# Masked attentions of a two-block transformer: TensorE takes the units of work in twos

## The chip, the cores and the metric

The program runs on one core of one Trainium2 chip. The metric is the device time of one execution, in microseconds (us). Five engines work beside each other, each through its own list of instructions in order, and they wait for one another by counting semaphores: TensorE (PE; its weight loads are shown apart as PEld), VectorE (DVE), ScalarE (ACT), GpSimd (POOL) and SyncE (SP, which issues DMAs).

## The reference, cut to what matters

Two transformer blocks run one after the other over 512 tokens of width 1024. Nearly all of their work is matrix products with weights. Two stages are masked attentions, and the change touches these alone. The first has 16 heads of 64 columns:

```
logit[t,s] = q_t.k_s / sqrt(d) + c[t] - c[s]   for s <= t, else -1e30
pr = softmax(logit);   o = pr @ v              # 512 tokens, 16 heads of 64
```

The second (`moba_attention`) has 8 heads of 64. At 512 tokens and blocks of 256 it comes to a plain causal softmax with a bias of slope times distance. A third attention, over a memory of 256 tokens and without a mask, has code of its own and is not touched.

## The kernel before, in words

A program writes the instruction list of each engine by hand. Weights come by DMA in slabs into `raw`. ScalarE rounds them to `w_hi`, GpSimd makes the rest `w_lo`, and TensorE does three products for each (lines 599 to 601). Outside the attentions TensorE is fed in this way without a break.

A masked attention is cut into units. Unit `i` is one pair of heads `j = i // 4` and one tile of 128 queries `qb = ROW_TILE[i % 4]`, with `ROW_TILE = (0, 3, 1, 2)`. As the mask is causal, its keys are the first `qb + 1` blocks of 128, so that units 0, 1, 2, 3 of a pair have 1, 4, 2 and 3 blocks. The first attention has N = 32 units and the second 16. Each unit has two halves, `hh` 0 and 1, one head each. Its way through the engines:

- `S_(i)` on TensorE (line 853): the scores of both heads, each on 64 rows of the array (line 863), then for each head a bf16 product that adds the mask (line 865) and tells `scored`. Odd units write banks 0 and 1 of `gp`, even ones banks 0 and 1 of `ms`. It waits until the maxima of unit i-2 are there (`biased`).
- `B_(s)` on VectorE (line 1897), for each half `s = 2 * i + hh`: bias added, row maximum taken. `E_(s)` on ScalarE (line 1346): exponential and row sum.
- `R_(i)` on VectorE (lines 1904 and 1908): reciprocal of the sums and scaling of both halves, which tells `weighted`.
- `T_(i)` on TensorE (line 874): for each half one transpose a block into bank 2 + hh of `ms`. Half 0 waits for `weighted` and until half 0 of unit i-1 was copied out of that bank; half 1 waits until half 1 of unit i-1 was.
- `C_(s)` on ScalarE (line 1354): that copy, into one of the four buffers `probT`.
- `V_(i)` on TensorE (line 885): the products with the values, each head on 64 columns of the array, after both copies of unit i. `H_(j)` and `L_(j)` on ScalarE and VectorE (lines 1358 and 1551) take a finished pair of heads out of PSUM.

What order VectorE and ScalarE keep is fixed and is not part of the change. VectorE does for each i: both `B_` of unit i, then `R_(i-1)`, and every fourth time an `L_`. ScalarE takes for each i the copies of unit i-3 and the exponentials of unit i in turn, half by half:

```
def C_(s):
    act.wait_ge(transposed, t0 + s + 1)
    if s >= 4:
        act.wait_ge(pv_done, at["pv"] + s // 2 - 1)
    act.activation(probT[s % 4][:, 0:w], ms[:, 2 + s % 2, 0:w], ACT.Copy).then_inc(pt_copied, 1)
for i in range(N + 3):
    for s in (2 * i, 2 * i + 1):
        if i >= 3: C_(s - 6)
        if i < N: E_(s)
    if i >= 8 and i % 4 == 0: H_(i // 4 - 2)
```

So ScalarE's order is C(u) half 0, E(u+3) half 0, C(u) half 1, E(u+3) half 1, and a copy of unit u waits also for `V_(u-2)`, which must have read the buffer that it overwrites. VectorE's `B_` of unit i waits in addition for the transposes of unit i-4, which read the place that it writes.

TensorE's order before is `S_(i)`, `T_(i-3)`, `V_(i-4)` for each i.

Of the kernel before, what the change touches and what calls it, by code (L numbers as in the profile page):

```python
# [116 lines left out]
def build(nc, hbm, out):  # L117
# [74 lines left out]
    with ExitStack() as ctx:  # L192
# [393 lines left out]
        def wait_evac(eng, pos, c):  # L586
            eng.wait_ge(evac[pos.slot(4, c)], pos.turns(4, c) + 1)
# [3 lines left out]
        def _(pe):  # L591
# [253 lines left out]
            def head_attention(at, n, queries, keys, values, before):  # L845

                t0, N = at["step"], 4 * n

                def S_(i):
                    j, qb = i // 4, ROW_TILE[i % 4]
                    w, bank = (qb + 1) * P, (ms, gp)[i % 2]
                    if i == 1:
                        for c in range(2):
                            wait_evac(pe, before, c)
                    if i >= 2:
                        pe.wait_ge(biased, t0 + 2 * i - 2)  # L860
                    for hh in range(2):
                        r = slice(64 * hh, 64 * hh + 64)
                        pe.matmul(bank[:, hh, 0:w], queries[r, j, qb * P:qb * P + P], keys[r, j, 0:w], start=True, stop=False)
                    for hh in range(2):
                        pe.matmul(bank[:, hh, qb * P:w], identb[:], tri[:], start=False, stop=True).then_inc(scored, 1)

                def T_(i):
                    for hh in range(2):
                        s = 2 * i + hh
                        pe.wait_ge(weighted, at["weighted"] + s + 1)  # L870
                        if i:
                            pe.wait_ge(pt_copied, at["pt"] + s - 1)
                        for kb in range(ROW_TILE[i % 4] + 1):
                            m = pe.transpose(ms[:, 2 + hh, kb * P:kb * P + P], prob_of[2 * ROW_TILE[i % 4] + hh][:, kb * P:kb * P + P], ident[:])
                        m.then_inc(transposed, 1)

                def V_(i):
                    j, qb = i // 4, ROW_TILE[i % 4]
                    pe.wait_ge(pt_copied, at["pt"] + 2 * i + 2)
                    if i % 4 == 0 and j >= 2:  # L880
                        pe.wait_ge(lo_done, at["split"] + j - 1)
                    for kb in range(qb + 1):
                        for hh in range(2):
                            c = j * P + 64 * hh
                            m = pe.matmul(gp[64 * hh:64 * hh + 64, 2 + j % 2, qb * P:qb * P + P], values[:, kb, c:c + 64],  # L885
                                          probT[(2 * i + hh) % 4][:, kb * P:kb * P + P], start=(kb == 0), stop=(kb == qb),
                                          skip_group_check=True)
                    m.then_inc(pv_done, 1)

                for i in range(N + 4):  # L890
                    if i < N:
                        S_(i)
                    if 3 <= i < N + 3:
                        T_(i - 3)
                    if i >= 4:
                        V_(i - 4)

            head_attention(fox, 8, qT, kT, v_s, Pos(gv["blk"] + 4))
            gemm(wo, A, ready=fox["split"])
            ffn_layer(1, B, A)  # L900
# [91 lines left out]
            slabs_wide(gvm, A, 0)  # L992
            branch(0, 0, lru["split"], 4)
            head_attention(mob, 4, qm, km, vm, Pos(br[0]["blk"] + 12))
            branch(1, 4, mob["split"], 4, late=2)
            first_blocks(wout, A, mrg["split"])
# [1312 lines left out]
```

## Time and profile before

| | |
|---|---|
| time, median of 3 runs | 2130.27 us (2128.96 to 2130.34) |
| span of the profiled execution (first to last instruction) | 2127.2 us |
| PE busy | 2098.9 us, 99% of the span |
| PEld / DVE / ACT / POOL busy | 1705.7 / 1014.4 / 805.4 / 936.1 us |
| mean granted TensorE clock | 0.997 of full speed |
| first masked attention, from its first score product to the first product of the next stage | 762.92 to 839.57 |
| second one | 1570.84 to 1612.62 |

The profile gives no time of its own for the profiled execution beside the span; what lies around the span is the difference to the runs, 3.1 us at the median. Busy time of PE is modelled at the ends of its instructions, so the distance from one start to the next is the surer measure of what a step takes. A time in brackets at the end of a row is the idle time of that engine ahead of the row, with what ended it.

### The profile page before, as it was taken

The page shows a single profiled execution, that of the slowest core. Times are in us where ns is not written, and L with a number is a line of the kernel's source. Part 1 is how long each engine was busy: PE and PEld are TensorE (multiplying, and loading weights), DVE is VectorE, ACT ScalarE, POOL GpSimd, SP SyncE. Part 2 cuts the span into 40 slices and gives each one's busy share as a digit, 9 for nine tenths or more (in the row PEclk, how much of TensorE's full clock was granted, in tenths as well). Part 3 has the DMA queues.
Part 4 walks back from the last instruction along what each step waited for, and adds up shares of the span by engine and source line. Part 5 has one row for each costly group of instructions (what it writes and reads, how often), then busy time and mean ns, then how long its engine had stood idle before and what let it go on. Part 6 is the DMA issues. An engine that isn't in the chain of part 4 may idle for free.

```text
span 2127.2 us, 26516 instructions
## 1 busy us (share of the span) xinstructions
PE 2098.9 (99%) x9908; PEld 1705.7 (80%) x9908; DVE 1014.4 (48%) x1580; ACT 805.4 (38%) x1243; POOL 936.1 (44%) x436
## 2 busy tenths in 40 slices
PE   9999999999999999999999999999999999999998
PEld 7777888888888866888888887878867888888887
DVE  7996623122356555532132355572454466254463
ACT  7766322122343157322222355352244343232232
POOL 5984544444444410444444442444443444444442
PEclk9999999999999999999999999999999999999999
DMA  5332432222222222232222221222211222322221
GB/s 193 133 115 79 145 113 82 96 100 97 99 81 99 100 90 90 80 117 81 100 97 99 99 91 49 104 82 98 98 60 60 99 90 97 106 84 100 97 99 60
DMA packets 33803, 205.31 MB, mean 97 GB/s; under 512 B 4512, under 2 KB 6688, under 8 KB 10672
## 3 DMA queue, kind: packets, MB, share of 16 engines
q1 hardware_dynamic: 33424, 199.87, 26.6%
q10 hardware_dynamic: 288, 4.19, 0.5%
q8 instruction: 60, 0.98, 0.2%
q14 instruction: 31, 0.25, 0.0%
HBM read 197.73 MB, written 6.32 MB: 96 GB/s over the span
## 4 chain that ended last, share of the span: by engine, by line
PE 60%; issue 23%; POOL 10%; DVE 5%; ACT 1%; DMA 0%; POOLq 0%; SPq 0%; DVEq 0%; ACTq 0%
PE gp L599 19%; PE gp L600 19%; PE gp L601 18%; POOL w_lo L493 9%; DVE ms L1554 3%; POOL pool_sum L516 1%; DMA h<-x_hbm 0%; PE gp L646 0%; PE gp L645 0%; PE gp L647 0%; PE ms L742 0%; PE ms L737 0%; PE gp L945 0%; PE gp L885 0%; DVE acc_sq L1551 0%
## 5 line engine op out<-in xcount | busy, mean ns | idle before, releaser
L493 POOL TENSOR_TENSOR w_lo<-raw,w_hi 128x1024 fp32r<-128x1024 f32 x350 | 848.0, 2426 | 1099.2 <-ACT w_hi L1071 1077.5
L599 PE MATMUL gp<-a_hi,w_hi 128*128 128x512 f32 (+1 forms) x1456 | 567.4, 390 | 1.8 <-DVE a_lo L1554 0.9
L601 PE MATMUL gp<-a_hi,w_lo 128*128 128x512 f32 (+1 forms) x1456 | 563.2, 387 | 0.0
L600 PE MATMUL gp<-a_lo,w_hi 128*128 128x512 f32 (+1 forms) x1456 | 563.1, 387 | 0.0
L1071 ACT ACTIVATE w_hi<-raw 128x1024 fp32r<-128x1024 f32 x349 | 365.5, 1051 | 505.9 <-PE gp L601 434.2
L600 PE MATMUL gp<-b_lo,w_hi 128*128 128x512 f32 (+1 forms) x1216 | 469.7, 386 | 0.0
L599 PE MATMUL gp<-b_hi,w_hi 128*128 128x512 f32 x1184 | 462.8, 391 | 0.0
L601 PE MATMUL gp<-b_hi,w_lo 128*128 128x512 f32 x1184 | 460.6, 389 | 0.0
L599 PEld LDWEIGHTS gp<-a_hi,w_hi 128*128 128x128 f32 x1456 | 273.5, 188 | 60.3 <-POOL w_lo L493 1.5
L600 PEld LDWEIGHTS gp<-a_lo,w_hi 128*128 128x128 f32 x1456 | 273.5, 188 | 56.5 <-issue 1.4
L601 PEld LDWEIGHTS gp<-a_hi,w_lo 128*128 128x128 f32 x1456 | 273.4, 188 | 55.5
L1551 DVE TENSOR_TENSOR h<-gp,h 128x512 f32<-128x512 f32 (+1 forms) x106 | 72.1, 681 | 424.4 <-PE gp L601 424.4
L600 PEld LDWEIGHTS gp<-b_lo,w_hi 128*128 128x128 f32 x1216 | 228.4, 188 | 47.2 <-issue 1.2
L599 PEld LDWEIGHTS gp<-b_hi,w_hi 128*128 128x128 f32 x1184 | 222.3, 188 | 47.5 <-issue 1.0
L601 PEld LDWEIGHTS gp<-b_hi,w_lo 128*128 128x128 f32 x1184 | 222.3, 188 | 46.0
L1551 DVE TENSOR_TENSOR T<-gp,rstd 128x512 f32<-128x512 f32 x136 | 93.8, 690 | 308.7 <-PE gp L601 306.4
L1554 DVE SCALAR_TENSOR_TENSOR ms<-u_pad,par,ms 128x512 f32<-128x512 f32 x176 | 120.1, 749 | 1.2 <-ACT ms L1144 0.4
L1080 ACT ACTIVATE sqb<-h 128x512 f32<-128x512 f32 x61 | 38.4, 631 | 130.2 <-DVE h L1551 116.3
L1554 DVE SCALAR_TENSOR_TENSOR T<-gpad,par,T 128x512 f32<-128x512 f32 x48 | 83.3, 1734 | 5.2 <-DVE T L2131 0.2
L1272 ACT ACTIVATE b_hi<-U 128x512 fp32r<-128x512 f32 x32 | 20.3, 634 | 121.3 <-DVE U L1554 121.3
L1272 ACT ACTIVATE a_hi<-U 128x512 fp32r<-128x512 f32 x32 | 20.3, 634 | 120.6 <-DVE U L1554 120.6
L516 POOL TENSOR_TENSOR pool_sum<-pool_sum,sqb 128x512 f32<-128x512 f32 x45 | 57.2, 1290 | 8.5 <-ACT sqb L1163 8.3
(333 smaller groups left out, 1829.0 us busy)
## 6 DMA issues: line engine op xcount, KB each, us to landing
raw<-w_hbm SPq DMA_DIRECT2D x176, 1024.0 KB, 4.8
proj_scratch<-kT ACTq DMA_DIRECT2D x2, 2048.0 KB, 6.7
fbias<-negc_scratch SPq DMA_DIRECT2D x16, 256.0 KB, 3.4
h<-x_hbm SPq DMA_DIRECT2D x4, 512.0 KB, 7.5
u_pad<-proj_scratch SPq DMA_DIRECT2D x1, 2048.0 KB, 10.1
big<-proj_scratch SPq DMA_DIRECT2D x1, 2048.0 KB, 8.7
out_hbm<-h SPq DMA_DIRECT2D x8, 256.0 KB, 2.2
mem_raw<-mem_hbm SPq DMA_DIRECT2D x1, 1024.0 KB, 12.5
```

The lines of the kernel that those rows point to most:

```text
L493: g.tensor_tensor(at(w_lo), src, f32(at(w_hi)), ALU.subtract).then_inc(w_lo_done, 1)
L516: g.tensor_tensor(pool_sum[:, s], pool_sum[:, s], product_at(i, s, t + 1), ALU.add).then_inc(pool_conv, 1)
L599: pe.matmul(o, wh, xh, start=start, stop=False)
L600: pe.matmul(o, wh, xl, start=False, stop=False)
L601: return pe.matmul(o, wl, xh, start=False, stop=stop)
L1071: act.activation(at(w_hi), src, ACT.Copy).then_inc(w_hi_done, 1)
L1080: act.activation(dst, h[:, c], ACT.Square).then_inc(sq_done, 1)
L1272: act.activation(H_[0][:, k], U[:, k % 2], ACT.Copy).then_inc(hi_done, 1)
L1551: return v.tensor_tensor(o, a, b, op)
L1554: return v.scalar_tensor_tensor(o, a, s, b, op0, op1)
```

## The change

Only TensorE's order of the calls changes; the calls themselves, their waits and the lists of the other engines stay.

```
-                for i in range(N + 4):
-                    if i < N:
-                        S_(i)
-                    if 3 <= i < N + 3:
-                        T_(i - 3)
-                    if i >= 4:
-                        V_(i - 4)
+                for i in range(3):
+                    S_(i)
+                for i in range(0, N, 2):
+                    T_(i)
+                    for a in (i + 3, i + 4):
+                        if a < N:
+                            S_(a)
+                    T_(i + 1)
+                    if i:
+                        V_(i - 1)
+                    V_(i)
+                V_(N - 1)
```

For even i the order is now `T_(i)`, `S_(i+3)`, `S_(i+4)`, `T_(i+1)`, `V_(i-1)`, `V_(i)`. Both masked attentions use this function.

## Rows read from the trace of the kernel before

**Rows 1.** Busy time of each engine by stretch: engine, busy us, instructions; granted clock; DMA.
```profile
762.92:839.57 76.65, 73.15 (x673) 45.72 (x672) 58.31 (x232) 63.77 (x200) 2.35 (x1) 1.00 0.13 43
1570.84:1612.62 41.78, 37.53 (x338) 22.90 (x337) 32.87 (x117) 31.25 (x99) 4.17 (x4) 1.00 0.01 2
762.90:772.00 9.10, 7.32 (x49) 3.57 (x48) 7.82 (x33) 7.49 (x24) 2.35 (x1) 1.00 0.10 33
2124.00:2127.20 3.20, 0.00 (x0) 0.00 (x0) 0.00 (x0) 0.00 (x0) 0.00 (x0) 0.88 0.74 250
```

**Rows 2.** Timeline of PE, first attention: start us, length us, engine, line, operation.
```profile
791.92 0.70 PE L863 MATMUL ms<-kT,qT 64*128 64x256 f32 x4
...
795.41 0.39 PE L874 MATMUL ms<-ident,T 128*128 128x128 f32 x2
795.73 0.88 PE L885 MATMUL gp<-sqb,v_s 128*64 128x128 f32 x12
796.53 0.49 PE L863 MATMUL ms<-kT,qT 64*128 64x128 f32 x4
796.96 0.29 PE L865 MATMUL ms<-tri,identb 128*128 128x128 bf16 x2
...
798.42 1.13 PE L863 MATMUL gp<-kT,qT 64*128 64x512 f32 x4
799.49 0.28 PE L865 MATMUL gp<-tri,identb 128*128 128x128 bf16 x2
799.61 0.61 PE L874 MATMUL ms<-ident,U 128*128 128x128 f32 x4
800.14 1.09 PE L885 MATMUL gp<-sqb,v_s 128*64 128x128 f32 x16
801.17 0.70 PE L863 MATMUL ms<-kT,qT 64*128 64x256 f32 x4
```

**Rows 3.** Timeline of the same stretch: ScalarE, one step of VectorE, one of PE.
```profile
792.17 0.72 ACT L1346 ACTIVATE T<-T,nmax 128x512 f32<-128x512 f32 x1 [1.00 <-DVE nmax L1897]
...
792.90 0.36 ACT L1354 ACTIVATE acc_sq<-ms 128x256 f32<-128x256 f32 x1
...
793.40 0.52 PE L874 MATMUL ms<-ident,T 128*128 128x128 f32 x3 [0.22 <-DVE T L1908]
...
794.73 0.48 ACT L1354 ACTIVATE sqb<-ms 128x384 f32<-128x384 f32 x1
795.10 0.51 ACT L1346 ACTIVATE U<-U,nmax 128x256 f32<-128x256 f32 x1
...
795.74 0.56 DVE L1897 CUSTOM_DVE_ANT_0 T<-gp,fbias 128x384 f32<-128x384 f32 x1 [0.58 <-PE ms L874]
...
796.34 0.62 ACT L1346 ACTIVATE T<-T,nmax 128x384 f32<-128x384 f32 x1 [0.34 <-DVE nmax L1897]
...
797.73 0.60 ACT L1354 ACTIVATE sqb<-ms 128x512 f32<-128x512 f32 x1
...
798.22 0.39 ACT L1346 ACTIVATE T<-T,nmax 128x128 f32<-128x128 f32 x1
```

**Rows 4.** Timeline of the first steps of the first attention.
```profile
763.34 0.29 PE L865 MATMUL ms<-tri,identb 128*128 128x128 bf16 x2
...
763.56 1.13 PE L863 MATMUL gp<-kT,qT 64*128 64x512 f32 x4
763.77 0.29 DVE L1897 CUSTOM_DVE_ANT_0 T<-ms,fbias 128x128 f32<-128x128 f32 x1
...
767.38 0.39 PE L874 MATMUL ms<-ident,T 128*128 128x128 f32 x2
...
767.72 0.49 PE L863 MATMUL ms<-kT,qT 64*128 64x128 f32 x4
```

**Rows 5.** Timeline of the last products with the values and the step after them.
```profile
838.77 0.88 PE L885 MATMUL gp<-sqb,v_s 128*64 128x128 f32 x12
...
839.69 0.60 ACT L1358 ACTIVATE a_hi<-gp 128x512 fp32r<-128x512 f32 x1 [0.98 <-PE gp L885]
```

## The prediction

> **What bounds the kernel now.** I read the busy times of the page first: PE is busy for 99% of the span, so that a change of TensorE's order counts one for one as soon as it opens a gap. Then the stretches of the two masked attentions [rows 1]: 76.65 us and 41.78 us, PE busy for 73.15 and 37.53 of them, with ACT at 63.77 in the first, which is close behind. Then the timeline of PE in the steady part [rows 2]: one pair of heads (four units) goes from the score product at 791.92 to the one at 801.17, 9.25 us. All other stages are untouched, and their weights are fetched ahead, so the whole difference must come from 12 such groups of four units, 8 in the first attention and 4 in the second.
>
> The prices of TensorE's steps, from start to start [rows 2]. Scores: 0.43 us for one block (796.53 to 796.96) and 1.07 for four (798.42 to 799.49), so 0.213 a block and 0.216 before the mask may start. Transposes of both halves: 0.32 for one block each (795.41 to 795.73), 0.53 for two, so 0.108 a transpose and 0.105 before the values start. Values: 0.80 for three blocks, 1.03 for four (800.14 to 801.17), so 0.213 a block and 0.17 after them. The two mask products: 0.11, and 0.01 to the transposes. Four units hold 10 blocks: scores 2.13, values 2.13, 20 transposes 2.16, eight mask products 0.44, together 6.86. The changes between kinds of products add 4 x (0.216 + 0.105 + 0.17 + 0.01) = 2.00. That is 8.86, and the missing 0.39 is a wait that the trace shows. At 793.40 half 1 of a three-block transpose starts after a gap [rows 3]. The row names a scaling on VectorE as the releaser, but that one was long done. What ended last is the copy of the unit before: the copy at 792.90 takes 0.36, and 0.11 later PE goes on. That copy stood behind the exponential of 792.17, and this behind a maximum of VectorE (1.00 idle, ended by it). This pattern decides the case: **ScalarE's half-1 copy of unit u stands behind the exponential of unit u+3**, so it needs the scores of unit u+3.
>
> **What the change does to TensorE alone.** No instruction is added or removed, no DMA is moved. Per two units the old order has S-mask, T-V and V-S twice each. The new one has S-mask twice, and T-S, mask-S, T-V and V-T once each. The trace shows mask-S: the mask at 763.34, the next score product at 763.56, so 0.22 less 0.11 for the mask, 0.11 [rows 4]. T-S it shows once, 767.38 to 767.72, 0.34 less two transposes, 0.12, where a wait may be in it; so it lies between 0 and 0.12, and I take 0.11, near the row. V-T I take as V-S, 0.17, between 0 and 0.2; it doesn't matter below, since a wait covers it. Per four units the changes then cost 0.86 + 0.22 + 0.22 + 0.21 + 0.34 + 0.02 = 1.87 in place of 2.00. So packing the like products together saves 0.13 us in four units, 1.6 us in all.
>
> The Trainium skill's page TensorEngine Tiling (Array Packing), section Tiling Modes, Key Properties, says that a change of the tiling mode, and not merely of the tile, drains TensorE. By its rule one counts borders between modes: the full-array mask stands between the two score products, so there are six borders per two units in the old order and six in the new, and the saving would be nothing in place of 1.6 us.
>
> **What it does to the waits.** Take the new order for even i: T(i), S(i+3), S(i+4), T(i+1), V(i-1), V(i), and write h0 and h1 for the halves.
>
> First, S(i+3) used to be issued ahead of T(i) and now comes after it. The copy of T(i) h1 stands behind the exponential of unit i+3, and T(i+1) h1 can't start before that copy. So PE, having done S(i+3), S(i+4) and T(i+1) h0, stands still until the way scores, maximum, exponential, copy has been walked through.
>
> Second, a copy of unit i+1 waits for V(i-1), and V(i-1) used to be issued ahead of T(i+1). Now it comes after it. So these copies can't begin while V(i-1) runs, and T(i+2), which comes next but for V(i), waits for both of them, with the exponential of unit i+4 h0 between the two.
>
> These two chains join end to end, and nothing of them runs beside itself. Prices: from the start of a mask to the maximum 0.43 (763.34 to 763.77, rows 4), taken as 0.44. From a maximum to its exponential its length and 0.11: 0.60 for three blocks (795.74 to 796.34, rows 3), 0.73 for four (VectorE steps grow by 0.13). An exponential holds ScalarE for 0.38, 0.49, 0.61, 0.72 by blocks. A copy holds it for 0.37 at three blocks (794.73 to 795.10) and 0.49 at four (797.73 to 798.22), taken as 0.48; with the time to PE it is its length (0.26, 0.38, 0.48, 0.58) and 0.11 [rows 3]. From the end of V to a copy 0.28: at 838.77 three blocks take 0.64, and ScalarE starts at 839.69 [rows 5]. I take it between 0.17, what PE itself needs after V, and 0.35, as much above.
>
> Now one period of four units, i = 0 mod 4, from the start of the h0 copy of unit i-1 (three blocks):
> - copy 0.37, exponential of i+2 0.49, h1 copy to PE 0.59, T(i) h1 and change 0.22, scores of i+3 (three blocks) 0.855, to the maximum 0.44, to the exponential 0.59, exponential 0.61, h1 copy of i (one block) to PE 0.37, T(i+1) h1 (four blocks) and change 0.535, V(i-1) three blocks 0.64, to the copy 0.28: 5.99 us;
> - h0 copy of i+1 0.48, exponential of i+4 0.38, h1 copy to PE 0.69, T(i+2) h1 and change 0.33, scores of i+5 (four blocks) 1.07, 0.44, 0.73, exponential 0.72, h1 copy of i+2 to PE 0.49, T(i+3) h1 and change 0.43, V(i+1) four blocks 0.85, 0.28: 6.88 us.
>
> Together **12.87 us in place of 9.25**. As a check from PE's side: 8.73 of work and changes, and waits of 0.27 and 0.75 at T(i), 0.81 at T(i+1) h1, 0.59 and 0.64 at T(i+2), 1.07 at T(i+3) h1, 4.13 in all. The other queues keep clear of this path: VectorE has some 7.3 us of work in a period and ScalarE 7.5, H and L among them. The bias DMAs are issued a head pair ahead, as now. With the two open prices at their ends (T-S 0 or 0.12, V to copy 0.17 or 0.35, each twice), the period is 12.4 to 13.0.
>
> Start and end, rolled forward by the same terms: T(1) h1 at 7.29 us after the first score product, V(0) at 7.82, T(2) h1 at 9.24 behind the copies, S(5), its maximum, its exponential and the h1 copy of unit 2, T(3) h1 at 13.01 and V(1) at 13.44. Six periods of 12.87, a last one of 9.89 (no scores are left to wait for), and 2.76 to the end: 103.3 us for the first attention. The old order rolled in this way gives 9.21 a period and 76.2 in all, where the trace has 76.65, which is the best proof that I have for the prices. So +26.7. The second attention: 13.44 + 2 x 12.87 + 9.89 + 2.76 = 51.8. Its old roll is 39.4 against 41.78 in the trace, so 2.4 us there are of another kind (VectorE still busy with the stage before as it starts, and longer waits behind it). They may stay (+12.4) or be swallowed by the new waits (+10.0); I take +11.0. Sum +37.7 us. On the span of 2127.2 that is 2164.9, and as the median of the runs stands 3.1 above the span, **2168**. Own range: twelve periods at 12.4 to 13.0 and the two ends of the second attention's start give 2161 to 2171.
>
> **Rivals.**
> *The waits are hidden and only the packing counts* (the other side). The mechanism sits at the copies: if ScalarE reached them without the exponentials between, PE would run at 8.73 in four units against 9.21 to 9.25, about 0.5 x 12 = 6 us less: 2124. It decides where the waits in a period fall below 0.5 us. For it: PE is 95% busy in the stage now, and ACT has slack. Against it: the wait of 793.40 arises already now, with S(u+3) issued ahead of T(u).
> *Only the first chain bites*, because the end of V(i-1) frees the buffer soon enough. The same roll without that wait gives 10.79 a period, 88.0 and 44.9 us: +11.4 and about +4, 2146. For it: the three blocks are a short product. Against it: the program's wait stands between them without anything to cover it.
> *The clock falls.* PE would be idle for a third of the stage, in gaps up to 1.1 us. At half the clock (1.2 GHz in place of 2.4) the TensorE terms on the path, some 4.5 us of a period, double: 17.4, +50 us more, 2218. Against it: from 762.90 to 772.00 PE was busy for 7.32 of 9.10 and the clock stayed at 1.00; the only drop is 0.88 in the last 3.2 us, with PE wholly idle [rows 1]. The Trainium skill, TensorE: Matmul & The Clock Gate, in its section on a second failure mode (psum-queue depth-cycling), tells of a kernel whose short idle times between groups of products made the clock swing; so far the trace doesn't bear that out.
>
> **How the numbers follow.** The forecast gets 0.82, the hidden waits 0.06, the first chain alone 0.07, the clock 0.05. The range of 2154 to 2182 holds the forecast's own range with a margin for prices that I have mis-sized by a third of the added waits, and leaves the rivals out. A difference of 0.2% (4.3 us) is what can be told from none. Faster: 0.04; same: 0.03; slower: 0.93.
>
> **What would show it.** Right: four units take 12.4 to 13.0 us in the steady part of both attentions; the transposes show idle PE ahead of h1 four times in a period, the longest, about 1.1, ahead of the three-block unit; ScalarE's copies after odd units start about 0.3 after the three- or four-block value product; the clock stays 1.00 and all other stages keep their length. Wrong: a period under 11 with copies that start ahead of V's end would leave the first chain alone; a period near 8.8 without waits, the packing; transposes that last twice as long, the clock.

## The result, and the profile after

The changed kernel takes 2172.49 us (median of 5 runs, 2171.84 to 2174.56) against 2129.49 us before (5 runs): ratio 1.0205, interval 1.0194 to 1.0216. It is 43.0 us slower, where I had forecast 37.7. The span of its profiled execution is 2170.7 us, 43.5 more than before. Instructions and bytes are the same in number. PE's busy time grew by 8.8 us all the same. The profile models the ends of its instructions, so that two transposes followed by a wait are shown as 0.41 us, though the next step could begin after 0.22; so part of each wait counts as busy, and a stretch at half clock in the second attention adds to it. The rest of the difference is idle time.

First the row of the page with the busy times (share of the span, number of instructions), then the two attentions and two short stretches of the second one by windows (stretch and length; busy us of PE, PEld, DVE, ACT, POOL; granted clock; DMA share and GB/s):

```profile
PE 2107.7 (97%) x9908; PEld 1708.8 (79%) x9908; DVE 1015.4 (47%) x1580; ACT 805.2 (37%) x1243; POOL 936.6 (43%) x436
```

```profile
762.84:869.20 106.36, 77.41 (x673) 46.89 (x672) 58.87 (x232) 63.65 (x200) 2.35 (x1) 1.00 0.09 31
1600.47:1655.87 55.40, 40.40 (x338) 23.89 (x337) 33.16 (x117) 31.26 (x99) 4.17 (x4) 0.97 0.00 1
...
1607.00:1611.00 4.00, 1.63 (x13) 0.83 (x11) 3.86 (x12) 2.95 (x10) 2.09 (x2) 1.00 0.01 4
1611.35:1614.82 3.47, 3.47 (x11) 1.15 (x10) 0.95 (x3) 0.39 (x2) 0.00 (x0) 0.51 0.00 0
```

Against the first two of [rows 1] the attentions are 29.7 and 13.6 us longer, 43.3 of the 43.5 us. Everything else kept its length to 0.3 us. VectorE and ScalarE did the same work (DVE 58.87 us against 58.31, ACT 63.65 against 63.77): the engines stand and wait for each other.

One period of four units in the first attention, from the timeline (start, length, engine, line; in brackets the idle time ahead and its releaser; line numbers of ScalarE and VectorE are 5 higher than before):

```profile
791.65 0.48 ACT L1359 ACTIVATE sqb<-ms 128x384 f32<-128x384 f32 x1
...
792.27 0.30 PE L874 MATMUL ms<-ident,T 128*128 128x128 f32 x1 [0.57 <-ACT sqb L1359]
...
792.50 0.92 PE L863 MATMUL gp<-kT,qT 64*128 64x384 f32 x4
793.35 0.28 PE L865 MATMUL gp<-tri,identb 128*128 128x128 bf16 x2
793.57 0.49 PE L863 MATMUL ms<-kT,qT 64*128 64x128 f32 x4
793.80 0.56 DVE L1902 CUSTOM_DVE_ANT_0 T<-gp,fbias 128x384 f32<-128x384 f32 x1 [2.93 <-PE gp L865]
...
794.40 0.61 ACT L1351 ACTIVATE T<-T,nmax 128x384 f32<-128x384 f32 x1 [1.61 <-DVE nmax L1902]
...
795.01 0.26 ACT L1359 ACTIVATE acc_sq<-ms 128x128 f32<-128x128 f32 x1
...
795.41 0.63 PE L874 MATMUL ms<-ident,T 128*128 128x128 f32 x4 [0.69 <-DVE U L1913]
...
795.97 0.88 PE L885 MATMUL gp<-sqb,v_s 128*64 128x128 f32 x12
...
796.96 0.60 ACT L1359 ACTIVATE sqb<-ms 128x512 f32<-128x512 f32 x1 [1.09 <-PE gp L885]
...
798.57 0.41 PE L874 MATMUL ms<-ident,U 128*128 128x128 f32 x2 [0.46 <-ACT sqb L1359]
...
798.91 1.13 PE L863 MATMUL gp<-kT,qT 64*128 64x512 f32 x4
...
802.38 0.52 PE L874 MATMUL ms<-ident,T 128*128 128x128 f32 x3 [0.94 <-DVE T L1913]
802.83 1.09 PE L885 MATMUL gp<-sqb,v_s 128*64 128x128 f32 x16
...
804.03 0.49 ACT L1359 ACTIVATE sqb<-ms 128x384 f32<-128x384 f32 x1 [1.09 <-PE gp L885]
...
804.91 0.48 ACT L1359 ACTIVATE sqb<-ms 128x384 f32<-128x384 f32 x1
```

The same copy comes again 13.26 us later (791.65 to 804.91), where [rows 2] had 9.25 us. The reader can walk both chains. First chain: the scores of 792.50 come after the transpose of 792.27. The maximum starts at 793.80 after VectorE had been idle for 2.93, the exponential at 794.40, the copy at 795.01, and the transposes of 795.41 had waited for that copy. The row names VectorE's scaling for it, wrongly, as it did before. Second chain: the values of 795.97, then the copy at 796.96, which names PE as its releaser (1.09 idle). In [rows 2, 3] no copy waits for values.

### The profile page after: what moved, and what is told of

The parts are those of the page before. It is cut to its first block, busy times and chain, and to the rows that moved or that the text cites. A ratio compares the mean times of both kernels' runs of the same rounds, so it can differ in the third digit from the quotient of the medians.

```text
span 2170.7 us, 26516 instructions
## 1 busy us (share of the span) xinstructions
PE 2107.7 (97%) x9908; PEld 1708.8 (79%) x9908; DVE 1015.4 (47%) x1580; ACT 805.2 (37%) x1243; POOL 936.6 (43%) x436
## 4 chain that ended last, share of the span: by engine, by line
PE 59%; issue 24%; POOL 10%; DVE 5%; ACT 1%; DMA 0%; POOLq 0%; SPq 0%; ACTq 0%; DVEq 0%
PE gp L599 18%; PE gp L601 18%; PE gp L600 18%; POOL w_lo L493 9%; DVE ms L1559 3%; POOL pool_sum L516 1%; PE gp L885 0%; PE gp L863 0%; PE gp L647 0%; PE gp L645 0%; PE gp L646 0%; PE ms L737 0%; PE ms L742 0%; DMA h<-x_hbm 0%; PE ms L874 0%
## 5 line engine op out<-in xcount | busy, mean ns | idle before, releaser
L874 PE MATMUL ms<-ident,T 128*128 128x128 f32 x192 | 33.7, 281 | 29.7 <-DVE T L1913 10.6
```

## The experiments

Each ratio is to the kernel before, with its interval. First four runs cut or keep one chain each. A border is a change from one kind of product to another on TensorE; "borders" is the rival by which the new neighbours on TensorE cost the time.

**Eight buffers.** The changed order, but the copies go into eight buffers in place of four; the four new ones are tiles of `rest_of_b` that are free in both attentions, and the products with the values read from the same eight.

```
+        probT8 = probT + tuple(rest_of_b[:, k] for k in range(4))
-                    if s >= 4:
-                        act.wait_ge(pv_done, at["pv"] + s // 2 - 1)
-                    act.activation(probT[s % 4]...
+                    if s >= 8:
+                        act.wait_ge(pv_done, at["pv"] + s // 2 - 3)
+                    act.activation(probT8[s % 8]...
```

> The changed order, but the copies go into eight buffers instead of four (the four new ones lie in memory that is free in both attentions), so that a copy of unit u waits for the values of unit u-4 and no longer for those of unit u-2. My theory (two chains end to end): the second chain is cut. ScalarE's copies of odd units start right behind the transposes, a period of four units goes from 13.26 to about 10.85 us, and the kernel to about 2148 us, 24 less than the changed one. Rival (the new borders between kinds of products on TensorE cost the time, not the waits): no product has moved, so nothing changes, 2172 us.

Measured: 2150.33 us (4 runs), 1.0101 (1.0085 to 1.0118), 22 us less than the changed kernel. The timeline, a period:

```profile
793.28 1.13 PE L864 MATMUL gp<-kT,qT 64*128 64x512 f32 x4
...
797.20 1.09 PE L886 MATMUL gp<-sqb,v_s 128*64 128x128 f32 x16
797.22 0.47 ACT L1360 ACTIVATE rest_of_b<-ms 128x384 f32<-128x384 f32 x1
...
801.94 0.63 PE L875 MATMUL ms<-ident,T 128*128 128x128 f32 x4 [0.70 <-DVE U L1914]
...
804.23 0.70 PE L864 MATMUL gp<-kT,qT 64*128 64x512 f32 x2
```

10.95 us from 793.28 to 804.23. The copy of 797.22 starts with the values of 797.20 and no longer behind them. The wait of the first chain (0.70 at 801.94) is untouched. No product of TensorE has changed its place in the order, so borders fall as a cause for these 22 us, half of the loss.

**Copies first.** The changed order with four buffers, but ScalarE takes both copies of a unit before both exponentials:

```
-                    for s in (2 * i, 2 * i + 1):
-                        if i >= 3:
-                            C_(s - 6)
-                        if i < N:
-                            E_(s)
+                    if i >= 3:
+                        C_(2 * i - 6)
+                        C_(2 * i - 5)
+                    if i < N:
+                        E_(2 * i)
+                        E_(2 * i + 1)
```

> The changed order, but ScalarE takes both copies of unit u before both exponentials of unit u+3, instead of in turn. My theory: the first chain is cut (the half-1 copy no longer stands behind an exponential that needs the scores of unit u+3), and the second one is shortened by the exponential between its two copies. A period of about 10.3 us, 2143 us. Rival (borders): 2172 us. Second rival (ScalarE's queue is not the cause, VectorE's scaling is, as the trace names it): 2172 us too, with idle PE named for VectorE as before.

Measured: 2141.68 us (4 runs), 1.0058 (1.0041 to 1.0075). What is left:

```profile
795.99 0.83 PE L874 MATMUL ms<-ident,T 128*128 128x128 f32 x6
...
800.80 1.04 PE L874 MATMUL ms<-ident,T 128*128 128x128 f32 x8
...
802.76 1.09 ACT L1359 ACTIVATE sqb<-ms 128x512 f32<-128x512 f32 x2 [0.36 <-PE gp L885]
...
803.50 0.90 PE L874 MATMUL ms<-ident,U 128*128 128x128 f32 x4 [0.63 <-ACT sqb L1359]
```

The odd units' transposes, six and eight in a row, now run without a gap between their halves: the waits of 0.94 and 0.69 that had VectorE's name are gone, though nothing of VectorE was changed. So it was the copy, and the name was wrong. The second chain stands (0.36 ahead of the copies, 0.63 on PE).

**Only the values in twos**, order `S_(i+3)`, `T_(i)`, `S_(i+4)`, `T_(i+1)`, `V_(i-1)`, `V_(i)`; **only the scores in twos**, order `T_(i)`, `S_(i+3)`, `S_(i+4)`, `V_(i-1)`, `T_(i+1)`, `V_(i)`:

```
                 for i in range(0, N, 2):
+                    if i + 3 < N:
+                        S_(i + 3)
                     T_(i)
-                    for a in (i + 3, i + 4):
-                        if a < N:
-                            S_(a)
+                    if i + 4 < N:
+                        S_(i + 4)
                     T_(i + 1)
```
```
+                    if i:
+                        V_(i - 1)
                     T_(i + 1)
-                    if i:
-                        V_(i - 1)
                     V_(i)
```

> Only the half of the change that puts products with the values together: S(i+3), T(i), S(i+4), T(i+1), V(i-1), V(i). My theory: the second chain stays and the first is shorter, as S(i+3) stands ahead of T(i) again: a period of about 11.2 us, 2151 us. Rival (borders between kinds of products): this order has five borders per two units against six in the kernel before, so it would be no slower than 2129.5 us.

> Only the half of the change that puts scores together: T(i), S(i+3), S(i+4), V(i-1), T(i+1), V(i). V(i-1) stands ahead of T(i+1) again. My theory: the first chain stays, the second goes: a period of about 10.8 us, 2147 us, near the run with eight buffers. Rival (borders): seven borders per two units, one more than the changed kernel, so slower than 2172 us.

Measured: values alone 2155.34 us (4 runs), 1.0121 (1.0104 to 1.0138); scores alone 2149.74 us (4 runs), 1.0099 (1.0082 to 1.0115). By borders the first (five in two units, where the kernel before has six) had to beat the kernel before, and the second had to be the slowest of all. (My expectation counts seven borders for it; there are eight, as both `T_` now stand behind a `V_`.) Neither is so. Each half alone costs 20 to 26 us, so each has its own chain. The scores alone, period 10.84 us as expected:

```profile
794.67 1.13 PE L863 MATMUL gp<-kT,qT 64*128 64x512 f32 x4
...
805.51 1.13 PE L863 MATMUL gp<-kT,qT 64*128 64x512 f32 x4
```

The values alone missed by 4 us, and the profiled run, with 2159.44 us the slowest of its four, by 8. Steady periods in its first attention are 11.29, as expected, or 12.9 (once 13.1). The timeline of such a longer one, and windows: the attention, one us of the longer period, and four us behind the same step of the next period, which is a short one:

```profile
786.38 0.52 PE L874 MATMUL ms<-ident,T 128*128 128x128 f32 x3 [1.65 <-DVE T L1914]
786.83 1.69 PE L885 MATMUL gp<-sqb,v_s 128*64 128x128 f32 x16
789.30 1.53 PE L863 MATMUL gp<-kT,qT 64*128 64x384 f32 x4
```

```profile
763.42:861.59 98.17, 80.81 (x673) 51.10 (x672) 58.31 (x232) 64.20 (x200) 2.35 (x1) 0.93 0.10 33
789.00:790.00 1.00, 1.00 (x6) 0.51 (x4) 0.00 (x0) 1.00 (x5) 0.00 (x0) 0.50 0.00 0
799.29:803.29 4.00, 4.00 (x42) 2.72 (x43) 2.51 (x10) 2.77 (x10) 0.00 (x0) 1.00 0.00 2
```

After the idle 1.65 us, from shortly after 787 until shortly before 791, the granted clock is at 0.50, the lower level of 1.2 GHz. The three-block scores take 1.46 to their mask (789.30 to 790.76) in place of 0.85. The mean over this attention is 0.93, against 1.00 in the changed kernel. The idle 1.65 us do not bring the fall each time: the same idle time stands ahead of 799.29 and of 823.49, and behind both the clock stayed at 1.00 for the next 4 us. In this trace four of the first attention's six idle times of 1.65 are followed by a fall, and two in the second attention. The longest idle times of PE in the changed kernel, in its first and in its second attention:

```profile
861.96 0.63 PE L874 MATMUL ms<-ident,T 128*128 128x128 f32 x4 [1.33 <-DVE U L1913]
...
1611.01 0.41 PE L874 MATMUL ms<-ident,U 128*128 128x128 f32 x2 [1.61 <-DVE T L1913]
```

The clock stayed at 1.00 behind the first and fell behind the second. In the run with the scores alone two idle times of 1.61 stand in the second attention, and only behind the later one did the clock fall. So each fall seen in the attentions came behind an idle time of about 1.6 us; what else decides is not shown.

**Both chains cut** in the changed order (both diffs above):

> The changed order with both chains cut: eight buffers for the copies, and both copies of a unit ahead of both exponentials. My theory (the two chains are the whole cost): what is left is the way from S(i+3), now behind T(i), to the transposes two units on; a period of about 9.5 us, 2134 us. Rival (borders between kinds of products): 2172 us less what the two runs alone gave (22 and 31 us), so if each takes its own piece 2119 us, and if they overlap as two chains that share the exponential do, my figure.

Measured: 2131.80 us (10 runs), 1.0011 (1.0002 to 1.0021), period 9.54 us. 40.7 of the 43.0 us are back, with TensorE's order as in the changed kernel. The two alone gave 22 and 31, 53 in sum: they overlap, as two chains that share an exponential must. What is left of the waits, from the timeline:

```profile
798.90 0.62 ACT L1352 ACTIVATE T<-T,nmax 128x384 f32<-128x384 f32 x1 [0.97 <-DVE nmax L1904]
...
800.11 1.06 ACT L1360 ACTIVATE sqb<-ms 128x512 f32<-128x512 f32 x2
...
800.83 0.90 PE L875 MATMUL ms<-ident,U 128*128 128x128 f32 x4
...
801.65 1.13 PE L864 MATMUL gp<-kT,qT 64*128 64x512 f32 x4
```

The copies of unit i+1 (800.11) still stand behind the exponentials of unit i+3 (798.90), whose scores now come after `T_(i)`. The transposes of 800.83 wait for these copies and take 0.82 us to the next scores, where four transposes and the change are 0.54 by the prices of the prediction. Such waits come to 0.8 us in a period, 9.54 against the 8.73 of work and changes (an estimate by the same prices). The profile shows only 0.3 of them as idle time (PE is busy for 9.24 us of 9.54), since the modelled ends of its instructions cover the rest.

**The kernel before with copies first; the values in twos with both chains cut:**

> The kernel before, with both copies of a unit ahead of both exponentials on ScalarE. My theory: the wait of some 0.4 us in a period that the order before has (half-1 copy behind an exponential) goes, a period of 8.86 in place of 9.24 us: 3.3 us less in the first attention and 1.8 in the second, 2125 us. Rival (PE is busy 99% and that wait costs nothing, or it comes back in another place): 2129.5 us.

> Products with the values in twos, score products one by one as before (S(i+3), T(i), S(i+4), T(i+1), V(i-1), V(i)), with eight buffers and copies first, so that both chains are cut. My theory: five borders per two units where the kernel before has six, and no waits: a period of about 8.55 us against 8.86 for the old order with copies first; 2121 to 2122 us, the best of all. Rival (packing brings nothing, since what a border costs is a wait for weights that is there either way): not under the run with copies first, about 2125 us.

Measured: 2122.63 us (6 runs), 0.9969 (0.9957 to 0.9981), and 2121.08 us (5 runs), 0.9958 (0.9945 to 0.9972). Periods from the timelines, first of the old order, then of the values in twos:

```profile
797.11 1.13 PE L863 MATMUL gp<-kT,qT 64*128 64x512 f32 x4
805.94 1.13 PE L863 MATMUL gp<-kT,qT 64*128 64x512 f32 x4
```

```profile
796.93 1.13 PE L864 MATMUL gp<-kT,qT 64*128 64x512 f32 x4
...
800.17 1.09 PE L886 MATMUL gp<-sqb,v_s 128*64 128x128 f32 x16
801.09 0.61 PE L886 MATMUL gp<-rest_of_b,v_s 128*64 128x128 f32 x8
801.31 0.84 ACT L1361 ACTIVATE rest_of_b<-ms 128x384 f32<-128x384 f32 x2
801.63 0.92 PE L864 MATMUL gp<-kT,qT 64*128 64x384 f32 x4
...
805.46 1.12 PE L864 MATMUL gp<-kT,qT 64*128 64x512 f32 x3
```

8.83 and 8.53 us. So the wait that the kernel before already had was worth 0.4 us a period, and packing the values 0.30 more. The second run has eight buffers besides, which were not tried alone in the old order; but the 8.83 us are already what the old order's steps come to without any wait (8.86 by the prediction's prices), so more buffers had nothing to give there. The run with the old order is 2.4 us faster than I expected (2125). Its first attention is 3.6 us shorter (73.08 us), where I expected 3.3, and its second 3.2 (38.53 us), where I expected 1.8. Six blocks of values take 1.46 us to the next scores (800.17 to 801.63): 1.28 of work and 0.18, where two single ones pay 0.17 each.

**The bias rows ahead.** My roll of the second attention missed 2.4 us. GpSimd makes four of its eight bias rows while it runs. In this run of the kernel before all eight are made ahead of it, and ahead of GpSimd's next slabs of weights:

```
-                if j >= 2:
-                    g.wait_ge(biased, mob["step"] + 8 * (j - 1))
-                    g.tensor_tensor(mbias[:, r % 4], dist[:], ...
+                    g.tensor_tensor(mbias[r], dist[:], ...   # r of 8, in kT and rest_of_b
```

> The kernel before, with all eight bias rows of the second attention made by GpSimd before it starts, in memory that is free then, in place of four before and four during it. It tests what the 2.4 us of another kind are that my roll of the second attention missed: in the trace before, VectorE's scaling takes 2.20 us in place of 0.62 where GpSimd makes a bias beside it. Theory: the two slow steps go, the second attention is about 1.5 us shorter, 2128 us. Rival: the steps were slow for another reason, 2129.5 us.

Measured: 2128.18 us (11 runs), 0.9993 (0.9984 to 1.0002): not told from no change. Two rows from the changed kernel, GpSimd's bias and VectorE's scaling of 256 columns, and four from this run, the same two with two products of VectorE between them:

```profile
1607.41 2.09 POOL L564 TENSOR_TENSOR mbias<-dist,par 128x512 f32<-128x512 f32 x2 [8.52 <-DVE nmax L1902]
1607.45 2.20 DVE L1913 TENSOR_SCALAR U<-U,rinv 128x256 f32<-128x256 f32 x2
```

```profile
1562.65 1.04 POOL L562 TENSOR_TENSOR rest_of_b<-dist,par 128x512 f32<-128x512 f32 x1
...
1567.23 2.17 DVE L1549 TENSOR_TENSOR merged<-merged,T 128x512 f32<-128x512 f32 x1
...
1572.83 0.69 DVE L1549 TENSOR_TENSOR merged<-merged,T 128x512 f32<-128x512 f32 x1
...
1578.90 0.61 DVE L1906 TENSOR_SCALAR U<-U,rinv 128x256 f32<-128x256 f32 x2
```

2.20 us against 0.61: the mechanism is shown. The second attention is 40.57 us long against 41.78, 1.2 us of the 2.4. The two slow steps were worth more: the second and third period lost 0.80 and 1.13 us, but the first grew by 0.74. For GpSimd's slabs now come later, and while it works on them (1563.64 to 1571.63) three of VectorE's products for the stage before take 2.2 to 2.7 us each, as the one at 1567.23, where the one behind them takes 0.69; so VectorE comes to the attention late. In the changed kernel the slow scaling also stands ahead of the longest idle time of PE (1611.01), and then comes the stretch at clock 0.51 in the windows above.

**The bias rows with each of the two faster orders:**

> The run with values in twos, eight buffers and copies first, and in addition the bias rows of the second attention made before it. Theory: the two gains are in different places and add up: 2121 less 1 to 2 us, about 2119.5 us, the best. Rival: in the freed order PE no longer waits for VectorE where GpSimd slows it, so the bias brings nothing, 2121 us.

> The kernel before with copies first and the bias rows made before the second attention; TensorE's order as before. Theory: 2122.6 less 1 to 2 us, about 2121 us, and 1.5 to 2 us above the run with values in twos, which is what packing the values is worth (0.3 us for each of 12 groups of four units, less what the longer start costs). Rival: packing is worth nothing, both runs the same.

Measured: values in twos 2119.97 us (5 runs), 0.9958 (0.9944 to 0.9972); old order 2123.54 us (8 runs), 0.9971 (0.9961 to 0.9982). The intervals overlap those without the bias rows, so the bias brings nothing that the times can tell. In the traces the second attention goes from 38.80 to 37.90 us with the values in twos and from 38.53 to 38.70 in the old order, so at best 0.9. The values in twos lie 1.6 and 3.6 us under the old order in two pairs of runs on one chip each; their intervals overlap, but the 0.3 us a period is plain in the traces. The fastest version is 9 us faster than the kernel before and 52 us faster than the change, and keeps one half of it.

## Why the prediction was right

The direction, the place and both mechanisms were right. 2172.5 us lies within the range of 2154 to 2182, though 1.5 above my own range of 2161 to 2171, as two waits were mis-sized and the clock fell once.

- *Four units take 12.87 us.* Measured 13.26. The order of waits is as predicted, with idle PE ahead of T(i+1) h1 0.69, T(i+2) 0.63 and 0.46, T(i+3) h1 0.94. Sizes were off: from the end of V to the copy 0.35 and not 0.28 (795.97 to 796.96 is 0.99, with 0.64 of work), twice 0.07. I had measured it where ScalarE's next step was H, not a copy. The way from a copy to PE is 0.14 and not 0.11 (795.01 to 795.41, 0.40 with 0.26 of copying), four times 0.03; [rows 3] had 0.14 too, as the copy of 792.90 ends at 793.26 and PE goes on at 793.40. The rest of the 0.39, 0.13, is spread over single hundredths. The first attention took 106.4 us where I had 103.3: six periods give 2.3 of the 3.1, the last, shorter one 0.26, the end 0.17. One period of the six is 13.53 us long, as a copy began 0.27 later behind its values (836.99); why is not shown.
- *The second attention, +11.0.* It was +13.6. The same 0.39 in each of four periods makes 1.6 of the 2.6, and the clock the other 1.0. From 1611.35 to 1614.82 PE took 3.47 us for two score products and what lies between and behind them, where other periods take 1.91 (798.91 to 800.82). Only the first product is on the path: it took 2.01 to its mask in place of 1.06, and the period grew by 1.0 (1611.35 to 1625.61, 14.26 us against 13.25 for the next). The rest fell into PE's wait at the transposes that follow, 0.39 in place of 0.94. Of the 2.4 us that the old roll had missed, the 1.0 that I kept did stay.
- *The rival of the clock*, with 0.05, did happen, but for 3.5 us and not for the stage, and cost 1.0 us in place of 50. The Trainium skill, TensorE: Matmul & The Clock Gate, section on the second failure mode, says that short idle times between groups of products can make the clock swing. Here the first attention of the changed kernel bears it out nowhere (1.00, with idle times of 0.94 in each period and one of 1.33), the run with the values alone does four times in that stage (0.93).
- *The first chain alone*, priced at 2146 us, is the run with eight buffers: 2150. It fell as a rival because the second chain was there, and the run shows that this chain hung on the copy's wait for the values alone: 10.95 us a period without it, where I had rolled 10.79.
- *The packing is worth 0.13 us in four units.* This stays an estimate: no run shows the changed order without waits. With both chains cut it takes 9.54 us, 0.7 more than the old order with one cut, but that holds the 0.8 us of waits that are left. What the runs do show is the values alone in twos, 0.30 us with the waits gone. The Trainium skill's page TensorEngine Tiling (Array Packing), section Tiling Modes, Key Properties, says that a change of the tiling mode drains TensorE. Counted by that rule the borders are six and six for the change and five for the values alone, and that this last order is the faster one once freed (8.53 against 8.83) agrees with it; whether six and six saves 0.13 or nothing no run shows.
- *Start and end* held within the same terms: T(1) h1, T(2) h1 and T(3) h1 of the first attention came 7.26, 9.21 and 13.02 us after its first score product, where I had 7.29, 9.24 and 13.01. Nothing outside the attentions moved.

## What to carry to other kernels

Grouping like instructions on one engine is an edit to a pipeline of four engines: before it, list for each moved instruction who waits for its result in strict order behind what. A change that looks local may take away the distance that kept two engines from waiting for each other. Here a roll of such a chain, made from start-to-start distances, gave the old time of the first attention to 0.6% (76.2 us against 76.65) and the new one to 3% (103.3 against 106.36); the terms that it mis-sized most stand in waits that only the new order has. And a queue that takes two streams in turn ties each to the slower one; let the one that another engine waits for go first, and then see whether packing pays. Here the first of these was worth 6.7 us without any packing.

## What I had not expected of the hardware

- VectorE's scaling of 256 columns, twice, took 2.20 us in place of 0.61 while GpSimd ran two products of 128x512 beside it, themselves 1.04 each, and a product of 128x512 took 2.17 in place of 0.69 beside GpSimd's slabs. So moving GpSimd's bias rows out of the attention moved the delay to its start.
- The granted clock fell to 0.50 behind idle times of 1.6 us, though not behind each of them, and stayed at 1.00 through a whole stage with idle times of 0.94 in each period and one of 1.33.
- The trace's releaser was wrong for the second halves of the odd units' transposes (0.69 and 0.94 us, put down to VectorE), which wait for a scaling and a copy; taking the copy out from behind the exponential removed these waits.
